# A hybrid attention layer on one core: the outputs of both groups of heads of every token tile multiplied in one run

## What is computed

```python
h = rms_norm(x, g_mix)
q_a, c_a, qi_a, ki_a, wi_a, q_b, kv_b, gate_b, gate_m = split_cols(h @ w_in, COL_SIZES)
o_a = dsa_mixer(...)   # 8 heads of 64; keys chosen by a top-128 over index scores
o_b = nsa_mixer(...)   # 8 heads of 64 in 2 groups of 4; compressed + selected + window attention
merged = sigmoid(gate_a_m) * (o_a @ w_up_a) + sigmoid(gate_b_m) * (o_b @ w_up_b)
x = x + merged @ w_out
x = x + square(relu(rms_norm(x, g_mlp) @ w_ff1)) @ w_ff2
# in each attention, for every head:
#   p = masked_softmax(q @ k.T * scale - slope * dist);  o = p @ v
```

## Time and profile before

| | |
|---|---|
| median of 3 runs | 748.39 us (748.23 to 749.61) |
| the profiled execution, its own time | 748.56 us |
| its span, first to last instruction | 746.8 us |
| PE busy | 737.7 us, 99% |
| DVE busy | 525.4 us, 70% |
| ACT busy | 416.6 us, 56% |
| POOL busy | 178.8 us, 24% |
| TensorE clock granted | 1.00 of full speed throughout |

### The profile page before, as it was taken

The page is one execution under the profiler, slowest core; times in us unless marked ns, Lnnn a source line. Parts: engine busy times, 40 slices in busy tenths (PEclk is TensorE's granted clock), DMA queues, the critical chain, the costliest instruction groups (busy, mean ns, idle before and its releaser), DMA issues.

```text
span 746.8 us, 11968 instructions
## 1 busy us (share of the span) xinstructions
PE 737.7 (99%) x4398; PEld 642.0 (86%) x4398; DVE 525.4 (70%) x999; ACT 416.6 (56%) x777; POOL 178.8 (24%) x192
## 2 busy tenths in 40 slices
PE   9999999999999999999999999999999999999998
PEld 9988977877997878777888899999998888888886
DVE  5478888779986977757668988988887544434443
ACT  7768377756678886664356565565565323232230
POOL 3110346424555553300023323222220000000000
PEclk9999999999999999999999999999999999999999
DMA  9622222111111021112632333333333232333322
GB/s 334 248 80 68 62 82 81 33 31 56 57 57 57 29 86 29 57 57 84 203 108 85 90 109 113 114 107 94 102 96 112 86 111 87 99 99 89 109 84 113
DMA packets 21833, 70.95 MB, mean 95 GB/s; under 512 B 2448, under 2 KB 3600, under 8 KB 21520
## 3 DMA queue, kind: packets, MB, share of 16 engines
q1 hardware_dynamic: 21776, 70.19, 30.2%
HBM read 68.08 MB, written 2.10 MB: 94 GB/s over the span
## 4 chain that ended last, share of the span: by engine, by line
PE 83%; DVE 8%; ACT 5%; issue 2%; DMA 2%; POOL 0%; SPq 0%; DVEq 0%
PE psum L1830 23%; PE psum L1832 23%; PE psum L1831 23%; PE psum L1838 5%; PE psum L2027 4%; PE psum L2004 2%; PE psum L2005 2%; DMA x2T<-in_xT 1%; DVE w_lo L1311 1%; ACT w_hi L929 1%; DVE x2T L1812 1%; DVE prob L1525 1%; ACT h L929 1%; ACT q_st L929 1%; DVE x2T L1678 1%
## 5 line engine op out<-in xcount | busy, mean ns | idle before, releaser
L929 ACT ACTIVATE w_hi<-stage 128x512 fp32r<-128x512 f32 (+4 forms) x149 | 118.3, 802 | 113.5 <-DMA stage<-in_panels 107.3
L1311 DVE TENSOR_TENSOR w_lo<-stage,w_hi 128x1024 fp32r<-128x1024 f32 (+4 forms) x74 | 76.4, 1037 | 110.1 <-ACT w_hi L929 105.8
L1830 PE MATMUL psum<-hT_hi,w_hi 128*128 128x256 f32 (+1 forms) x324 | 113.5, 350 | 1.0 <-DVE q_st L1467 0.6
L1831 PE MATMUL psum<-hT_lo,w_hi 128*128 128x256 f32 (+1 forms) x324 | 107.3, 331 | 0.0
L1830 PE MATMUL psum<-a_hi,w_hi 128*128 128x512 f32 x256 | 99.7, 389 | 0.2 <-issue 0.2
L1832 PE MATMUL psum<-a_hi,w_lo 128*128 128x512 f32 x256 | 99.6, 389 | 0.0
L1831 PE MATMUL psum<-a_lo,w_hi 128*128 128x512 f32 x256 | 99.6, 389 | 0.0
L1832 PE MATMUL psum<-hT_hi,w_lo 128*128 128x512 f32 (+1 forms) x264 | 90.6, 343 | 0.0
L1116 ACT ACTIVATE prob<-prob,neg_max 128x128 f32<-128x128 f32 (+3 forms) x96 | 53.8, 560 | 34.5 <-DVE neg_max L1525 33.8
L893 POOL TENSOR_TENSOR w_lo<-stage,w_hi 128x512 fp32r<-128x512 f32 x46 | 59.8, 1304 | 36.7 <-ACT w_hi L929 36.7
L1830 PE MATMUL psum<-t_hi,w_hi 128*128 128x256 f32 x240 | 67.9, 283 | 0.0
(11 more groups left out here) (276 smaller groups left out, 1708.9 us busy)
## 6 DMA issues: line engine op xcount, KB each, us to landing
stage<-in_panels SPq DMA_DIRECT2D x104, 512.0 KB, 3.6
xT_in<-in_xT SPq DMA_DIRECT2D x8, 260.0 KB, 4.9
x_in<-in_x SPq DMA_DIRECT2D x4, 512.0 KB, 7.1
phi<-in_phi SPq DMA_DIRECT2D x2, 1024.0 KB, 6.4
x2T<-in_xT SPq DMA_DIRECT2D x1, 2048.0 KB, 9.2
out_xT<-x2T SPq DMA_DIRECT2D x8, 256.0 KB, 2.0
stage<-in_panels SPq DMA_DIRECT2D x8, 212.0 KB, 4.9
stage<-in_panels SPq DMA_DIRECT2D x4, 408.0 KB, 3.1
```

The source lines that it names most:

```text
L929: return nc.scalar.activation(dst, src, ACT.Copy, scale=scale)
L1311: tt_op(w_lo[:, p % SLOTS, cols], stage[:, p % SLOTS, cols], hi_place(p)[:, cols].bitcast(F32), ALU.subtract)\
L1830: mm(dst, a_h, b_h, start=start, stop=False)
L1831: mm(dst, a_h, b_l, start=False, stop=False)
```

## The change

The step `pv` of a group was emitted as soon as its four units were through, except in tiles 0 and 1, where the first group was held back by four units and multiplied right ahead of the second. Now this holds for all four tiles.

```diff
         if u >= PV_LAG and (u - PV_LAG) % G == G - 1:
             n = (u - PV_LAG) // G
 
-            if n // 2 % TT > 1:
-                step("pv", n)
-            elif n % 2:
+            if n % 2:
                 step("pv", n - 1)
                 step("pv", n)
```

## The result

The changed kernel takes 751.39 us, the median of 7 runs (751.07 to 751.74), against 748.98 us (748.09 to 749.61, 7 runs) for the kernel before on the same chip. The ratio is 1.0037, 95% interval 1.0027 to 1.0046, so 2.0 to 3.4 us slower. The forecast had 749.5 us and 748.0 to 751.2: the sign of the sum was right, its size was less than half of what came, and the range missed by 0.2 us.

The account below looks back on a forecast made before the run. PE, 99% busy, was taken to bound the kernel except where DVE sets the time in the first branch. Places 1 to 6 summed 1.71 - 0.13 - 0.12 + 0.37 - 0.37 - 0.37 = +1.09 us: 749.5, range 748.0 to 751.2.

Parts of the forecast that it names:

- What bounds the kernel: Whole kernel: PE, busy 99% of the span, moves the end wherever it does not wait; DVE sets one first-branch stretch.
- what a step costs alone and joined: At the six places: x12 alone 1.65 us, joined 1.28; x16 alone 2.08, joined 1.71; each place gives back 0.37.
- The exit's 0.20: Product behind a lone first step takes 0.43 us instead of 0.23; this 0.20 was counted as saved at each place.
- place 6: Tile 3 of the third branch: no producer within reach holds PE, so the gain arrives, -0.37 us.
- Place 2: Tile 3 of the first branch: PE loses its 2.08 us lead waiting for cmp_e, then pays the joined step, +1.71 us.
- Places 1, 3 and 4: First branch tile 2, second branch tiles 2 and 3: PE waits 0.24, 0.25, 0.74 us; net -0.13, -0.12, +0.37.
- The `probT` wait: Behind joined steps: ACT's copy into probT waits some 1.8 us, costed at nothing because PE is busy meanwhile.
- Rival D: Slower: DVE and ACT chains hold PE at place 5 too, +1.28 instead of -0.37 us, 751.2; chance 0.14.
- place 5: Tile 2 of the third branch: DVE follows PE nearly all the way, so the gain arrives, -0.37 us.

Follow-up runs that it names:

- e4: Kernel before with only place 2 joined, its whole first step also kept and multiplied again in the joined step: 750.36 us against 748.75, ratio 1.0023.
- e7: Kernel before with only place 2 joined, a quarter of its first step also kept and multiplied again: 750.79 us against 748.74, ratio 1.0024.
- e1: Kernel before with only place 2 joining its two steps, the other five places as before: 751.50 us against 748.75, ratio 1.0035.
- e5: As e1, with one top-k round on DVE moved from unit 30 to unit 36, behind cmp_e: 751.50 us, ratio 1.0030 to the kernel before.
- e9: As e1, with POOL waiting for DVE's cmp_p before it subtracts panel 25: 749.31 us against 748.71 for the kernel before, ratio 1.0005.
- e10: As e9, with the top-k round moved as in e5 too: 748.24 us against 748.71 for the kernel before, ratio 0.9996.
- e3: Kernel before with only places 5 and 6 joined (tiles 2 and 3 of the third branch): 748.37 us, ratio 0.9996 to the kernel before.

## Why the prediction missed

- **What bounds the kernel, and what a step costs alone and joined:** right. A gain of 0.37 a place was forecast, and 0.35 and 0.31 came where PE kept its lead. The exit's 0.20 was taken for all six, which at place 6 is a little too much: four transposes behind that step take 0.59 in the kernel before, where four take 0.44. The Trainium skill, "TensorEngine Tiling (Array Packing)", Key Properties, and the traces agree in kind.
- **Place 2, the step that failed:** "PE will stand there ... for all of its 2.08 us, ... At 181.79 it is where it was, and then the joined step takes 1.71 us more. Result: +1.71." The wait came at its place and in its size (2.05, named to DVE), and the joined step cost 1.69. But "it is where it was" is false: it assumes that PE goes on behind the wait at the rate that it had. From about 1 us behind the wait it went on at half the clock; between 177 and 181 us that cost 1.6 us, of which 0.5 came back, since PE no longer waited for `fac`. So place 2 cost 2.81, and the missing term is 1.1 us. e4 shows the place without wait and without the term, e7 shows that the shorter wait does not have it, and the two kinds of runs of e1 and e5 show it in one program. No term and no rival of the prediction spoke of the clock, although the page of before ("1.00 throughout") only said what holds while PE hardly waits.
- **Why PE had to wait there:** right that DVE's work does not follow PE, but "its rows follow each other without a gap" was read as DVE's own work. Two of its rows were long because POOL was reading: 1.49 us at 173.88, where line 1606 takes 0.43, and 0.60 us at 172.79 for line 1604, which takes 0.17 in the other tiles. e9 and e10 show it. It did not change the sum, but it hid the way out. A third row of that stretch looks the same: line 1596 takes 1.05 us at 168.66, 0.42 in the three other tiles, and ends 0.28 behind a POOL multiplication (168.15 to 169.43). It is still 1.06 in e9 and e10, and no run took it away.
- **Places 1, 3 and 4:** the terms were mis-sized by 0.02, 0.16 and 0.09 us. At 3 and 4 the mechanism was right. Counted from the product ahead of `qa_n` to the one behind it, PE slid back 0.37 for 0.25 and 0.81 for 0.74; the rest, 0.04 and 0.02, lies in the steps, which cost a little less where they left and a little more where they joined than counted. At place 3 ACT's rounding starts at 234.18, late by just what PE was late ahead of the place (3.40), so it is set by earlier work as forecast; the excess is in the two handovers behind it, 0.10 from ACT to DVE's line 1465 and 0.15 from there to PE, where the working had 0.03 (no row of it shows that) and 0.10. At place 1 the size is right partly by luck: of the 0.22, 0.10 come at the transposes of `cmp_e`, which the forecast passed over (DVE is done with them at 150.49 and PE would want them at 152.15 - 1.65 = 150.50), and only the rest at line 2079, where all 0.24 were expected.
- **The `probT` wait, costed at nothing:** right. ACT in the changed kernel stands for 2.29 us behind place 2's step, where 1.8 were forecast, and PE starts its next product without a wait:

```profile
185.52 0.28 ACT L927 ACTIVATE probT<-psum 128x128 f32<-128x128 f32 x1 [2.29 <-PE psum L2025]
```

- **Rival D** names nearly the time that came (751.2), by a mechanism that did not happen: PE did not wait at place 5. The range was too narrow on its upper side, because the price of place 2 had no upper bound of its own. The working also stood on three runs of the kernel before and on a profile with the quickest start; the medians since are 748.7 to 749.0 instead of 748.39.

## What to carry to other kernels

Work taken away ahead of a wait is not only worth nothing: the idle time that is left may cost the clock behind it (here 1.91 us did in most runs, and 1.12 us in none). Price such a new wait of PE also with the matmuls that follow it at the lower clock, and fill it or shorten it. A chain without gaps is not a chain of its engine's own work: compare the length of each row with the same line elsewhere before believing that it bounds anything. And when an edit at a suspected cause brings nothing (e5), look at whether its instructions merely became longer.

## What the hardware showed unexpectedly

- PE's granted clock went from 1.00 to 0.50 (2.4 to 1.2 GHz) behind 1.91 us of idle time in the profiled runs of the changed kernel, e1 and e5. The clock over the span, 0.997 or 0.998, tells the same of all 7 runs of the changed kernel and 9 of the 13 of e1 and e5; it stayed at 1.00 behind 1.12 us in all 11 of e7. In the changed kernel it was back at 1.00 by 181 us. The Trainium skill, "TensorE: Matmul & The Clock Gate", section What's actually happening, describes a clock that follows how busy PE has been recently; the trace agrees with that. Its remark there that one kernel gets more or fewer slow matmuls from run to run is made of a kernel's start; the two kinds of runs of e1 and e5 show the like in mid-kernel.
- A DVE `tensor_tensor` with both inputs in SBUF took 1.19 (e5) or 0.62 us (e1) for 8 values a partition while POOL ran a subtraction, and 0.17 with POOL kept away (e9); a 128x256 one took 1.43 against 0.42. The Trainium skill, "SBUF — State Buffer", section Who interferes with whom, says that such an instruction contends with a GpSimd instruction that reads SBUF; the traces agree. DVE's line 1527 of e9, which reads PSUM and one SBUF tensor, keeps its 0.29 us beside POOL's subtraction.
- The first large matmuls of the kernel take 0.98 (e1) to 1.61 us (e3) for the same four, from one execution to the next, at a recorded clock of 1.00.
